# Second gate copied out with its sigmoids batched, 22 convolution taps ahead of the attention slots, group maximum a slot later, turned probabilities copied ahead of the next exponents

## The reference, cut to what matters

```python
def trunk_layer(x, conv_past, ffn_past, attend, p):
    xn = rms_norm(x, g_attn)
    a_in, q, k, v, qi, ki, wi, ga, gb = split_in(xn @ w_in)
    glu = a_in[..., :D_CONV] * jax.nn.sigmoid(a_in[..., D_CONV:])
    glu_ext = jnp.concatenate([conv_past.astype(glu.dtype), glu], axis=1)
    h = layer_norm(causal_dwconv(glu_ext, conv_w, conv_b), ln_g, ln_b)
    y_a = jax.nn.silu(h) @ w_a_out
    ...
    o = attend(q, k, v, qi, ki, wi)          # 256 best keys per token, softmax, 8 heads
    y_b = o.reshape(b, t, D_ATTN) @ w_b_out
    x = x + (jax.nn.sigmoid(ga) * y_a + jax.nn.sigmoid(gb) * y_b) @ w_o
    ...
```

## Time and profile before

| | us |
|---|---|
| median of 3 runs | 1437.95 |
| lowest, highest | 1432.43, 1440.23 |
| the profiled execution: its time | 1431.12 |
| the profiled execution: its span | 1429.0 |
| PE, DVE, ACT, POOL busy in the span | 1266.1, 752.9, 286.2, 204.6 |
| mean granted PE clock, as a share of 2.4 GHz | 0.913 |

### The profile page before, as it was taken

How to read it: one execution, slowest core, us unless ns; L and a number is a source line. 1 busy time by engine, 2 the same in 40 slices (tenths; PEclk the granted TensorE clock), 3 DMA queues, 4 the chain that set the end, 5 groups by cost and what they waited for, 6 DMA issues and landing times. The chain is left out here.

```text
span 1429.0 us, 17511 instructions
## 1 busy us (share of the span) xinstructions
PE 1266.1 (89%) x7043; PEld 990.3 (69%) x7043; DVE 752.9 (53%) x1723; ACT 286.2 (20%) x526; POOL 204.6 (14%) x210
## 2 busy tenths in 40 slices
PE   6989999987886899879637989999999999999996
PEld 3556763335774677656314447788999999998996
DVE  5112134998889872976864231312766666661220
ACT  2122223110001001332202220022222222232111
POOL 0010000001001121363774410000000000000111
PEclk9989985999998899987667879999999999999998
DMA  5232320113030213453764610620233333222330
GB/s 170 89 122 67 140 73 1 41 43 102 1 118 1 104 49 98 132 172 119 211 203 124 236 30 32 181 62 0 60 89 89 89 89 89 80 61 76 103 108 27
DMA packets 107020, 131.54 MB, mean 92 GB/s; under 512 B 8095, under 2 KB 76087, under 8 KB 105894
## 3 DMA queue, kind: packets, MB, share of 16 engines
q1 hardware_dynamic: 91830, 80.21, 18.4%
q0 software_dynamic: 14384, 48.62, 11.0%
q10 hardware_dynamic: 725, 1.60, 0.4%
HBM read 124.86 MB, written 5.54 MB: 91 GB/s over the span
## 5 line engine op out<-in xcount | busy, mean ns | idle before, releaser
L707 PE MATMUL G<-xnT,wring 128*128 128x280 f32 x768 | 206.7, 429 | 11.0 <-DVE gluT L1387 11.0
L1173 PE MATMUL G<-xnH,whi 128*128 128x274 f32 x704 | 205.2, 291 | 0.7 <-DVE aext L1667 0.7
L1174 PE MATMUL G<-xnL,whi 128*128 128x274 f32 x704 | 203.5, 289 | 0.0
L1175 PE MATMUL G<-xnH,wlo 128*128 128x274 f32 x704 | 202.9, 288 | 0.0
L707 PEld LDWEIGHTS G<-xnT,wring 128*128 128x128 f32 x768 | 154.8, 205 | 49.9 <-DVE gluT L1387 11.4
L699 PE MATMUL G<-wring,xnT 128*128 128x512 f32 (+3 forms) x400 | 158.2, 552 | 0.7 <-ACT srel L1803 0.7
L1174 PEld LDWEIGHTS G<-xnL,whi 128*128 128x128 f32 x704 | 133.4, 189 | 0.1
L1173 PEld LDWEIGHTS G<-xnH,whi 128*128 128x128 f32 x704 | 132.4, 188 | 1.0 <-issue 0.9
L1175 PEld LDWEIGHTS G<-xnH,wlo 128*128 128x128 f32 x704 | 133.1, 189 | 0.0
L1628 DVE TENSOR_TENSOR wlo<-wraw,whi 128x2048 fp32r<-128x2048 f32 (+1 forms) x38 | 76.4, 2011 | 93.3 <-ACT whi L1936 92.6
L699 PEld LDWEIGHTS G<-wring,xnT 128*128 128x128 f32 (+1 forms) x400 | 66.6, 185 | 77.8 <-issue 76.8
(11 more groups left out here) (361 smaller groups left out, 1964.8 us busy)
## 6 DMA issues: line engine op xcount, KB each, us to landing
wraw<-in_w_up_dram SPq DMA_DIRECT2D x44, 512.0 KB, 5.2
wring<-in_w_in_dram SPq DMA_DIRECT2D x9, 2048.0 KB, 7.8
wraw<-in_w_down_dram SPq DMA_DIRECT2D x16, 704.0 KB, 4.6
qB<-scr_q SPq DMA_DIRECT2D x32, 256.0 KB
wring<-in_w_o_dram SPq DMA_DIRECT2D x2, 2048.0 KB, 8.7
toep<-scr_toep SPq DMA_DIRECT2D x1, 2432.0 KB, 9.2
wring<-in_w_in_dram SPq DMA_DIRECT2D x2, 1024.0 KB, 9.3
wring<-in_w_a_out_dram SPq DMA_DIRECT2D x1, 2048.0 KB, 8.0
```

Of the source, the lines that this page charges most:

```text
L707: last = pe.matmul(out[:, i, 0:b - a], w[:, j, c:c + P], x[:, j, a:b], start=(j == 0), stop=(j == k - 1))
L1173: pe.matmul(out, w_hi, x_hi, start=start, stop=False)
L1174: pe.matmul(out, w_hi, x_lo, start=False, stop=False)
L1175: return pe.matmul(out, w_lo, x_hi, start=False, stop=stop)
```

## The change

Five edits, all in the attention stretch:

1. ACT takes the second gate out of its bank with Copy in place of Sigmoid. The eight sigmoids are done in place in one row after slot 39; each counts up a new semaphore `gb_open`, on which the product with `yb` now waits.
2. The two reductions of a key product become one over both blocks, and DVE no longer waits for its end.
3. 22 of the 62 taps are done before `at_max(0)`; the other 40 are spread over slots 0 to 28.
4. `group_max` and the group's exponents get a table of their own, one slot after `group_logits`; `group_prob`, `group_probs`, the quads and `group_out` of the second group move one slot later; of the first group only `group_prob` moves (14 to 15).
5. ACT copies `pT` of slot a before the exponents of slot a+1.

```diff
-    AT_WEIGHTS, AT_PROBS, AT_OUT = {14: 0, 27: 1}, {17: 0, 28: 1}, {25: 0, 36: 1}
-    AT_QUADS = {18: 0, 20: 1, 22: 2, 24: 3, 29: 4, 31: 5, 33: 6, 35: 7}
-    TAPS = (KC - PE_CONV) * CONV_W
+    AT_MAX, AT_WEIGHTS, AT_PROBS, AT_OUT = {14: 0, 27: 1}, {15: 0, 28: 1}, {17: 0, 29: 1}, {25: 0, 37: 1}
+    AT_QUADS = {18: 0, 20: 1, 22: 2, 24: 3, 30: 4, 32: 5, 34: 6, 36: 7}
+    TAPS, TAPS_FIRST = (KC - PE_CONV) * CONV_W, 22
...
-        return min(TAPS, TAPS * (a + 1) // 29)
+        return TAPS_FIRST + min(TAPS - TAPS_FIRST, (TAPS - TAPS_FIRST) * (a + 1) // 29)
...
-            for c in range(2):
-                last = dve.tensor_reduce(lgat[:, g, c, col:col + 8], x[:, c, :].rearrange("p (h d) -> p h d", d=64), AX.X, ALU.add)
-                if c == 0:
-                    step(last)
-            step(last, S["qk_done"])
+            step(dve.tensor_reduce(lgat[:, g, :, col:col + 8], x[:, :, :].rearrange("p c (h d) -> p c h d", d=64), AX.X, ALU.add), S["qk_done"], free=True)
...
         dve.wait_ge(S["st_done"], 2 * KC)
+        for i in range(TAPS_FIRST):
+            conv_tap(i)
         dve.wait_ge(S["toep_loaded"], 16)
         at_max(0)
...
-            if a in AT_LOGITS:
-                group_max(AT_LOGITS[a])
+            if a in AT_MAX:
+                group_max(AT_MAX[a])
...
-            freed(dve, ("gb", n))
+            dve.wait_ge(S["gb_open"], n + 1)
...
-            dst = m1 if kind == "ga" else sgb
-            step(act.activation(dst[:, n, :].rearrange("p (i t) -> p i t", i=2), src[:, :, 0:HALF], ACT.Sigmoid), free, free=True)
+            dst, how = (m1, ACT.Sigmoid) if kind == "ga" else (sgb, ACT.Copy)
+            step(act.activation(dst[:, n, :].rearrange("p (i t) -> p i t", i=2), src[:, :, 0:HALF], how), free, free=True)
...
+
+        def group_exp(g):
             act.wait_ge(S["grp_max"], g + 1)
...
             if kind == "gb":
                 gate(kind, n)
-            if a + 1 < ATTEND:
-                at_exp(a + 1)
             act.wait_ge(S["at_trans"], a + 1)
...
             step(last, S["at_pT"], free=True)
+            if a + 1 < ATTEND:
+                at_exp(a + 1)
             if h == 0 and r:
                 take_out(r - 1)
             if a in AT_LOGITS:
                 group_scale(AT_LOGITS[a])
+            if a in AT_MAX:
+                group_exp(AT_MAX[a])
...
+        for n in range(KM):
+            freed(act, ("gb", n))
+            step(act.activation(sgb[:, n, :], sgb[:, n, :], ACT.Sigmoid), S["gb_open"], free=True)
         take_out(NT - 1)
```

More of the change, by code:

```diff
@@ L460, in build_in @@
         relpad_done prompt_mask newhot_loaded f_high f_split xn2_val xn2_high hf_high hf_split dn_half
-        relpad_loaded dve_tap diag_w_ready diag_used qis_clear""".split()
+        relpad_loaded dve_tap gb_open diag_w_ready diag_used qis_clear""".split()
     S = {n: sem(n) for n in names}
```

## The result

In the first comparison the changed kernel took 1386.75 us (median; 1382.86 to 1393.34) against 1435.19 for the kernel before: 0.9665 of its time, 95% interval 0.961 to 0.972, **48 us faster where 21.4 were forecast**, and outside the stated range. The profiled execution took 1382.86 us, its span 1381.0, 48.0 less than before. In two later comparisons, on other chips, the same kernel stood at 0.978 (0.970 to 0.986) and 0.981 (0.977 to 0.985), 27 to 31 us faster by these ratios; what was different there is told with experiment 6. One of its 12 executions took 1625.8 us, at a mean granted clock of 0.72, and is left out of every ratio.

A forecast was written before the change was run, and what follows sets the result against it. PE was held by waits behind gate products and lowered clock, then by POOL's gathers, then by waits and half clock in slots 27 and 34. Terms -16 - 1 - 4.4 = -21.4 took 1437.95 to 1416.5 us; range 1403 to 1430.

The forecast's parts named there:

- Loads and copy: Slots after second-gate products: without table loads and with pT copied earlier, 1.35 us saved a gate, seven times, 9.5 us.
- A: Slots 0 to 14, the eight second-gate products, 558 to 677.5 us: 16 us faster, range 9 to 22.
- Sigmoids in a row: After slot 39: one load and eight activations, 6.4 us, hidden in ACT's 7.23 us idle time; cost nothing.
- Taps and reductions in A: Slots 8 to 10: less DVE work recovers 2 us of the 3.72 us by which a key's gather is late.
- group maximum in slot 14: Slots 13 and 14: taking the group's maximum and exponents off the path saves about 2.6 us.
- Clock in A: Eight second-gate products: fuller PE clock saves 2 us, between 0 and 7.3, because DVE then sets the pace.
- Part B: Slots 15 to 24, to 758 us: fewer taps beside POOL's gather issues save 1 us, between 0 and 2.4.
- Part C: 758 to 888 us: slot 27's wait, the quads' move and the clock together give -4.4 us, from +2 to -11.
- Quad 6 behind the norm: Slot 34: the quad now follows PE's layer-norm wait, +3.6 us, less 1.7 for an earlier pT, net +1.9.
- The clock returns in full: Rival, slots 0 to 14 and after 758 us: full PE clock returns, -33 us, 1405 us; chance 0.13.
- DVE and the gathers set A's pace: Rival, from slot 8: PE gains only what POOL's gather chain gains, -9 us, 1429 us; chance 0.14.
- Slower: Rival, slots without a filling product: the turn, copy, exponents ring outlasts PE's slot, +9 us, 1447 us; chance 0.06.

The follow-up runs named there:

- experiment 6: The changed kernel, unaltered, timed on two more chips (0.978 and 0.981 of the kernel before), plus two versions with extra filling matmuls in slot 27 (0.9792 and 0.9726).
- b_e15: The kernel before with edits 1 and 5 only; slots 0 to 14 took 104.3 us against 115.9.
- a_no3: The changed kernel without edit 3, all 62 taps in slots 0 to 28; 0.9828 of the kernel before, slots 0 to 14 in 95.2 us against 92.7.
- a_gap27: The changed kernel with the second group's maximum and exponents put back in slot 26; 0.9802 of the kernel before.
- a_q33: The changed kernel with the second group's third quad put back in slot 33; 0.9806 of the kernel before, the changed kernel beside it 0.9781.
- a_keys12: The changed kernel with keys 10 and 11 gathered ahead of POOL's wait for the fourth second-gate product; 0.9676 of the kernel before, slots 0 to 14 in 85.8 us.
- a_again: The changed kernel unaltered, timed again on another chip; 0.9781 of the kernel before.
- a_third: The changed kernel unaltered, timed a third time on a further chip; 0.981 of the kernel before.

## Why the prediction was wrong, step by step

**Loads and copy (9.5).** Near in size, not in its parts. The wait behind a gate fell from 2.22 to 0.45 us, 1.77 where 1.35 stood, but in `b_e15` PE then waited for DVE instead, and its idle time in A fell by 6.8 us only. With 4.8 of clock, which had its own term here, edits 1 and 5 won 11.6. The price of a load holds: each takes 1.28 us in the traces with the next instruction 0.01 to 0.02 behind. The drain that the Trainium skill (ScalarE: Activation LUTs, What ACT_TABLE_LOAD costs) adds shows in no row. The 0.3 given back per gate was too much: no turn waits there in the changed kernel.

**Sigmoids in a row (0), gap ahead of slot 0 (4.8 left).** Right: they end 1.3 us ahead of need, and the gap is 5.44.

**Taps and reductions in A (2), group maximum in slot 14 (2.6).** Taken out of the changed kernel, edit 3 is worth 2.5, near its term, and edit 4 5.4, twice its term, 3.2 of it clock. As terms of a sum both are wrong: alone neither moves A by more than 0.4 us. The merged reduction takes 1.22 instead of 1.41, close to the 0.2 taken; edit 2 was not run by itself, so what it gives to the whole is open.

**Clock in A (2, up to 7.3): the step that failed.** It came out at 11.1. Two errors made it. First, I counted only the eight products; the clock also falls on the turns, logits and weighted sums between them, and PE's whole busy time is what shrinks. The products gave 5.1 of it (66.1 us in all against 71.2 of the earlier trace rows), the other instructions 6. Second, the bound "DVE sets the pace at 10.8 us a pair" came from rounding up: three keys and three taps a pair. The tables give 4/3 of a key and 40/29 of a tap a slot, so 2.7 and 2.8 a pair. Keys at 2.4 us (1.22 + 1.22 less the overlap), 2.67 of them, 2.76 taps at 0.97 and two heads at 0.25 make 9.6 us, under the 9.85 that PE takes at full clock. The bound was not there. Even with all 62 taps, 4.3 a pair and 11 us on DVE by the same count, `a_no3` lost 2.5 us in A. And the bound as it stood, 0.8 us a pair, allowed 5.6 over seven pairs: the 2 was chosen, not worked out.

**Part B (1, up to 2.4).** Came out at 5.5: 3.8 of the gathers' chain and 1.7 because the fourth quad ran at full clock, which it does not always do in this kernel. On the kernel before, edit 3 alone gives 3.6 of the chain, above the end that I had given it; without it the changed kernel still keeps POOL's issues short (`a_no3`), so the split over the edits is open. The rule in the Trainium skill (SBUF — State Buffer, section "Who interferes with whom"), by which a `tensor_tensor` does not hold up descriptor writing, is not borne out by the means of B: 1.36 us an issue beside line 1554, 0.95 without. The same section has a DVE instruction with two SBUF inputs contend with a GpSimd instruction that reads SBUF; no run here shows whether a gather's issue is one.

**Part C (4.4, up to 11): the second failed step, again the clock.** C1, C2 and C3 together gave 18.5. The wait of slot 27 went, as forecast. But the half clock behind it was priced at 2 of at most 7, while `a_gap27` shows 9.8 us of PE time behind one wait of 1.8. I had counted only the 16 us that read 0.50; the slots before and behind them ran below 1.00 too. Of the 18.5 some 3 are the remote wait in the trace of before and not the change's. Quad 6 behind the norm cost at most 1 us and not 3.6. In `a_q33`, with the quad ahead of it, the wait in slot 34 was 5.5 us and not 8.3, and the slot behind it ran at half clock (its weighted sum 1.44 us, against 0.87 where the quad stood there); that the two make up for each other is my reading.

**The rivals.** "The clock returns in full" was the one that happened, and its gain of 33 us was 15 short of the 48: 2 in A, 4.5 in B, 7.5 in C (3 of these the remote wait of before), 1 ahead of A. Its C of 11 was also more than its own terms give (4.3 - 1.9 + 7 = 9.4). It had 0.13. "DVE and the gathers set A's pace" fell with its arithmetic; the late key it named was real, and `a_keys12` shows its price, 7 us. "Slower" didn't occur: the ring of turn, copy and exponents stayed hidden, with PE waiting for exponents 2.7 us in all, 2.3 of them ahead of A as before. On the two chips of `a_again` and `a_third` the gain of 27 to 31 us was near the forecast's 21.4, but that was luck: it came for a reason that the prediction didn't have: A won 7 us more than forecast there too, and what C had won was lost again behind late hand-overs.

## What to carry to other kernels

Price a wait of TensorE at its length plus what the work behind it costs at half clock: here 1.8 us of wait cost 11.6, and a fill of repeated matmuls in such a wait won 7 us net. That is an upper price, not a rule for every wait: edit 5's short waits in A cost no clock, and the fourth quad ran at either level behind waits of 2.3 to 3.1 us. So give every removed wait a term for the clock with a range that starts at nothing, take its upper end over all of PE's instructions in the stretch, from a stretch of the same trace that runs at full clock, and find out with one filled wait where in the range you are. And where several waits sit in one loop, price the edits together: in A edits 3 and 4 gave at most 0.4 us alone, edits 1 and 5 gave 11.6, all together 23.2.

## What the runs showed of the hardware that I had not expected

- A wait of 1.78 us in slot 27 was followed by PE work at 1.2 GHz for about 20 us (granted clock 0.50 from 746 to 766 us); the same slots without that wait ran at 2.4 GHz throughout (C1 34.8 against 23.2 us). Waits of 2.60 and 2.75 us ahead of the fourth quad left it at 2.4 GHz, one of 2.29 us in another execution of the same kernel did not.
- Hand-overs from PE to ACT came 1.6 to 8.2 us late in some traces, up to seven times in one execution, with waits of the same kind on DVE and POOL, and not once in others. In `a_again` and `a_third` the stretches B to C3, where they lie, took 20 us more than in the first trace of the changed kernel; the whole spans are 24 and 19 us longer. That the late hand-overs cause this is likely and not shown by a run.
- In B before, POOL's issue of a gather took 0.95 us with neither of DVE's two-input operations beside it, 1.10 beside a tap and 1.36 beside the product of line 1554.
- One reduction over 128 x 1024 takes 1.22 us where two over 128 x 512 take 1.41.
